# Experts of a mixture layer: the scatter of the block before goes ahead of the gathers three blocks on

## The reference

```python
def step(acc, inp):
    tok, w, e = inp
    xb = xf[tok]
    hid = silu(xb @ wg[e]) * (xb @ wu[e])
    yb = (hid @ wd[e]) * w[..., None]
    acc = acc.at[tok.reshape(-1)].add(yb.reshape(-1, D_MODEL))
    return acc, None
```

## Time and profile before

| | us |
|---|---|
| median of 3 runs | 2062.29 (2060.82 to 2064.68) |
| the profiled execution's own time | 2062.23 |
| its span | 2060.5 |
| PE busy | 1992.8 (97%) |
| DVE busy | 1139.9 (55%) |
| POOL busy | 778.1 (38%) |

### The profile page before, as it was taken

How to read it: one execution, slowest core, us unless ns; L and a number is a source line. 1 busy time by engine, 2 the same in 40 slices (tenths; PEclk the granted TensorE clock), 3 DMA queues, 4 the chain that set the end, 5 groups by cost and what they waited for, 6 DMA issues and landing times.

```text
span 2060.5 us, 23760 instructions
## 1 busy us (share of the span) xinstructions
PE 1992.8 (97%) x7237; PEld 1013.2 (49%) x7238; DVE 1139.9 (55%) x3065; ACT 504.8 (24%) x1102; POOL 778.1 (38%) x717
## 2 busy tenths in 40 slices
PE   8999999999999999999999999999999999999992
PEld 6444667575544444444445554444444444444440
DVE  6222546776621222335676656966666666666645
ACT  3111554452322222314432230111111111111113
POOL 1762005622122221115980002554545545455541
PEclk9999999999999999999999999999999999999996
DMA  5421000011132222144353006999999999999964
GB/s 148 133 86 41 21 21 22 22 47 47 46 129 76 72 82 77 54 123 171 103 207 140 37 31 258 362 361 349 357 359 352 358 358 352 355 349 351 358 206 172
DMA packets 129639, 370.45 MB, mean 180 GB/s; under 512 B 33712, under 2 KB 65668, under 8 KB 103832
## 3 DMA queue, kind: packets, MB, share of 16 engines
q1 hardware_dynamic: 103960, 314.83, 40.8%
q0 software_dynamic: 23520, 54.61, 10.9%
q10 hardware_dynamic: 2080, 0.01, 0.1%
HBM read 320.57 MB, written 68.17 MB: 189 GB/s over the span
## 4 chain that ended last, share of the span: by engine, by line
PE 40%; DMA 7%; POOL 3%; issue 3%; DVE 2%; ACT 0%; SPq 0%; POOLq 0%; DVEq 0%
PE banks L3192 17%; PE banks L3208 8%; DMA sums<-arena,row_to 6%; PE banks L2289 4%; PE banks L2336 3%; POOL arena L2136 2%; PE banks L2014 2%; PE banks L2352 1%; PE banks L279 1%; PE banks L2803 1%; PE banks L2312 1%; PE banks L3200 1%; DMA arena<-in_w_router_dram 0%; DVE arena L3268 0%; DVE arena L3185 0%
## 5 line engine op out<-in xcount | busy, mean ns | idle before, releaser
L3192 PE MATMUL banks<-arena 128*128 128x512 f32 x1056 | 468.8, 597 | 3.3 <-DVE arena L3185 0.8
L3171 POOL DMA_INDIRECT arena<-h_rows,index x268 | 280.0, 1045 | 140.4 <-issue 77.8
L3192 PEld LDWEIGHTS banks<-arena 128*128 128x128 f32 x1056 | 195.2, 190 | 226.3 <-issue 224.8
L1720 PE MATMUL banks<-arena 128*128 128x512 f32 x672 | 299.0, 594 | 1.1 <-ACT arena L323 1.1
L3208 PE MATMUL banks<-arena 128*128 128x512 f32 x528 | 237.6, 593 | 1.3 <-ACT arena L3007 0.8
L3179 POOL DMA_INDIRECT sums<-arena,row_to x66 | 108.0, 1636 | 272.2 <-DMA sums<-arena,row_to 231.9
L3185 DVE STREAM_TRANSPOSE arena<-arena 128x1024 f32<-128x1024 f32 x66 | 133.9, 2029 | 119.8 <-PE banks L3192 115.1
L279 PE MATMUL banks<-arena 128*128 128x512 f32 x416 | 191.8, 598 | 2.5 <-PEq L108 2.2
L1720 PEld LDWEIGHTS banks<-arena 128*128 128x128 f32 x672 | 123.1, 190 | 135.6 <-issue 134.0
L3155 DVE TENSOR_SCALAR index<-row 32x1 uint32<-32x1 f32 x1072 | 155.4, 145 | 17.1
L3208 PEld LDWEIGHTS banks<-arena 128*128 128x128 f32 x528 | 100.2, 190 | 127.0 <-issue 125.3
(11 more groups left out here) (400 smaller groups left out, 2431.9 us busy)
## 6 DMA issues: line engine op xcount, KB each, us to landing
arena<-in_w_exp_gate_dram SPq DMA_DIRECT2D x66, 1024.0 KB
arena<-in_w_exp_up_dram SPq DMA_DIRECT2D x66, 1024.0 KB
arena<-in_w_exp_down_dram SPq DMA_DIRECT2D x66, 1024.0 KB
arena<-in_w_in_dram SPq DMA_DIRECT2D x26, 1024.0 KB, 5.3
gates<-arena SPq DMA_DIRECT2D x60, 256.0 KB, 2.0
arena<-gates SPq DMA_DIRECT2D x15, 1024.0 KB, 7.7
arena<-h_rows,index POOLq DMA_INDIRECT x268
arena<-in_x_dram SPq DMA_DIRECT2D x8, 512.0 KB, 5.8
```

What stands on the lines that cost most here:

```text
L1720: mm = pe.matmul(gate_bank(n, b), left[:, k, :], right[:, k, :], start=(alone and k == 0), stop=(k == 3), skip_group_check=True)
L3171: return pool.indirect_dma_start(w.x[k][:, 256 * q:256 * (q + 1)], None, rows, bass.IndirectOffsetOnAxis(ap=g.index[:, k, q:q + 1], axis=0 ...
L3192: mm = pe.matmul(g.bank[:, 2, :].rearrange("p (a f) -> p a f", a=2), xT[:, k, :], wgu[:, :, k, :], start=(k == 0), stop=(k == KT - 1))
```

## The change

In each step of the experts POOL issues S(c-1) first and G(c+3) after it. Every wait stays with its instruction, and no other engine's order changes.

```diff
             def step(i, c):
+                if has(i, c, -1):
+                    scatter(i, c - 1)
                 if has(i, c, 3):
                     gather(i, c + 3)
-                if has(i, c, -1):
-                    scatter(i, c - 1)
```

## The result

The changed kernel takes 2077.12 us (median of 4 runs, 2074.02 to 2080.53), the kernel before 2062.19 in the same comparison: the ratio is 1.0071, with a 95% interval from 1.0052 to 1.0091. It is slower by 14.9 us. I had predicted +3.2 us and a range that ended at 2071.0.

What follows compares the result with a forecast made beforehand. PE sets the pace with DMA full, and the chains through PE and scatters end almost together. A 5.05 us stop less 1.0, 0.5 and 0.4 gives +3.15 us, predicted 2065.5 us, range 2060.0 to 2071.0.

Steps and rivals of the forecast that it cites:

- the stops don't add up over the blocks: Experts' end: late gathers stop PE for 5.05 us, building up from about block 52; a late PE finds the next gather in place.
- s: How far the scatters move ahead by starting once R(0) is done, carried along the chain: 4.4 us, from 3.3 to 4.8.
- theory D: From the experiments, not the prediction: scatters' chain is slightly slower than PE; the order sets how much PE is spared.
- The floor of the lag: Least time from the start of R(b) to the start of S(b): R's own 0.75 us plus 0.30, some 1.05.
- my own formula: Around block 31: a gather takes the next one's old place, s earlier; T(31) has 8.75 us against a landing of 8.0.
- My first rival: Gathers fall back by nearly a whole step, as s comes out small: slower, +7.5 us, 2069.8; chance 0.34.
- The 0.84 us by which VectorE may be late: Harmless lateness of VectorE, from the hidden product's end at 1624.06 to the transposes at 1624.90; taken off a 5.89 us delay.
- my signs of being wrong: T waits for gathers early, lag of S shrinks under 3 us, T(60) doesn't wait, or steps around 1600 aren't 11.1 us.
- 8.0 us from the end of the last gather's issue to T: Landing time of a gather in full queues, taken near the upper end between 4.5 and 8.84 us.
- the third rival: The scatter chain alone sets the end and gives all of s: faster, -4.4 us, 2057.8; chance 0.06.
- The terms given back: Near the end: 1.0 us at down(59) to up(61), 0.5 slack between R(65) and S(65), 0.4 from weights served sooner.

Runs made afterwards that it cites:

- with the collisions taken away: The changed kernel, with VectorE's selection for block c+4 put ahead of the index work for c+3: 2074.94 us, ratio 1.0056 to the kernel before.
- selection first: The kernel before (old order), with VectorE's selection for block c+4 put ahead of the index work for c+3: 2063.52 us, ratio 1.0004.
- removed in either of two ways: The changed kernel with VectorE's selection put ahead of the index work, 2074.94 us, or with the selection split into four instructions, 2078.32 us.
- The old order with two sums: The kernel before, with odd blocks' scatters to a second sums tensor and each scatter waiting for the one two blocks back: 2062.30 us, ratio 0.9995.

## Why the prediction was wrong

**What bounds the kernel: right, and read too narrowly.** PE and the chain of scatters end almost together. I said so for the tail and used it to cap the gain. What the old trace also said is that the chain runs at 11.18 us per block (S(7) to S(51)) against PE's 11.08 (R(7) to R(51)), and that the old order hides this in a lag that may grow to some 12 us.

**The step that failed: "the stops don't add up over the blocks, since each gather's time hangs on the scatters' chain and not on PE".** The sentence is true of the waits, and I drew from it that the chain would keep its old pace, so that everything after could be read off the old trace, shifted by s. The chain did not keep it: 11.38 us per block after, 11.29 with the collisions taken away, while three kernels with the old order in the loop had 11.18, 11.14 (selection first) and 11.11 (new order at the ends). That is 8.6 of the 11.7 us lost between block 7 and block 51. So a chain that is a little slow by itself, as theory D has it, accounts for the smaller part; the larger is that it runs slower still in the new order. The runs show what it takes: the full weight loads (with five eighths of the down loads the loss is gone), the wait of each scatter for the one before (without it the loss is gone), and more than one gather between the scatter and the next.

**s, the shift of the scatters, was mis-sized.** I took 4.4 us from a range of 3.3 to 4.8. Measured at block 7, the lag shrank from 5.85 to 3.34, by 2.5, and in absolute time S(7) came only 1.3 us earlier. S(1) did start 2.9 us earlier (1315.58 against 1318.46), but took 4.14 us to issue instead of 1.60: line 2649 had held up a gather before (3.42 us at 1314.74), and now held up the scatter. The floor of the lag is 1.6 us, seen at S(1) (1315.58 against R(1) at 1313.98), and not 1.05. By my own formula the gathers of the middle, with 0.75 us to spare at s = 4.4, were then late by more than 1 us, so T had to wait from the start. My first rival named that condition, s below 3.4, and gave it 0.34; its price, +7.5 us, rested on the same unchanged chain and was half of what came. The 0.84 us by which VectorE may be late were too many as well: at 1415.92 the hidden product had ended 0.34 us ahead of the transposes, which started in time, and the matmuls of line 2803 behind them still took 0.75 us more than usual. Two of my signs of being wrong came true: T waited for gathers early, and the lag at block 7 shrank by less than 3 us.

**The room.** Old order: a lag of up to 12 us before PE is stopped. New order: between 1.8 and 6.5 us from block 7 to 51, 3.34 at the first and 4.89 at the last. When the lag grows, a gather comes late, PE is set back, and the lag starts to grow again. From S(35) to S(47) it was 1.8 to 3.5 us, and T waited for none of the gathers behind them, those of blocks 39 to 51. So PE is tied to the scatters in bouts, not block by block, and over the 44 blocks it is spared 3.1 us less drift.

**What held.** I had taken 8.0 us from the end of the last gather's issue to T. At the 19 places where T waited for a gather in the changed kernel it was 7.9 to 8.9 us, 8.3 in the mean. R's waits for landings vanished. The end of the kernel moved with PE and not with the scatters. No gain came, though the chain that ended last ran through the scatters; the third rival was rightly small. The terms given back (1.0, 0.5 and 0.4 us) can't be seen one by one beside a loss of this size, and no run tested them.

**The Trainium skill's rules.** The Trainium skill's "DMA: Bandwidth & Descriptors", section "Rules for kernel authors", says to issue a DMA early and wait for it late; the runs bear it out with a measured slope, +1.6, +6.8 and +14.9 us for one, two and four gathers put behind a wait. The Trainium skill's fit on the same page, section "Anatomy of one DMA", for a DMA from GpSimd gives an estimate of 2.3 us for one gather's bytes. It is not met: the median from issue to landing was 6.7 us in the changed kernel and 5.6 with a quarter of the down loads.

**What stays open.** Why the chain of scatters takes 0.1 us per block more when PE moves in step with it, with the collisions removed (11.29 against 11.18), no run separates. Late weights are hardly the cause: in the changed kernel the three loads of an expert land 9.4, 14.1 and 7.6 us after their issue (medians), and they are issued four blocks, some 45 us, ahead. With the collisions the chain's loss lies in the issues (9.8 us more from S(7) to S(51)); with them removed in either of two ways it lies in landing and restart (426.2 us instead of 419.9). Both pay nearly the same in the end, which looks like a pace that the coupled loop sets and not the scatter alone; that is a guess.

No version tried beats the kernel before by more than its measurement can tell.

## What to carry to other kernels

Where a chain of waits runs at nearly the pace of the bounding engine, ask how far it may fall behind before that engine must wait, and let no reordering use up that room: here 12 us of room hid a chain that was 1% too slow, and some 4 us did not. Do not read the new schedule off the old trace by a shift; once two loops are coupled, the slower one's pace becomes both's, and it may change. An operation whose start hangs on a DMA's landing is a bad thing to put ahead of work that is needed on time.

## What the hardware showed

GpSimd's issue of an indirect DMA is held up by VectorE's selection (tensor_tensor, 128x1024, float32 in, bf16 out, 1.23 us) if it begins while that runs: 2.65 us instead of 1.61. It is not if the issue began before it. The only exception in the changed kernel's trace is S(15), whose issue began 0.03 us into the selection and took 1.62 us. The tensor_tensor of line 2649 (128x3072, float32) held up S(1) in the same way, and in the kernel before a gather, for 3.42 us instead of 1.0. The index work of line 3155 (32x1 each) had no such effect: S(4), issued amid it at 1352.09, took 1.60 us.

TensorE's clock fell for a moment after some short pauses. After, the windows around S(34) (length, busy and count per engine, clock, DMA, GB/s):

```profile
1680.00:1690.00 10.00, 8.97 (x21) 3.61 (x19) 5.39 (x18) 1.07 (x2) 4.46 (x4) 1.00 1.01 367
1690.00:1700.00 10.00, 9.43 (x25) 4.61 (x26) 5.06 (x24) 0.38 (x1) 5.07 (x5) 0.83 1.02 371
```

A granted clock of 0.83 over 10 us means a part of them at the lower level, 1.2 GHz. It followed a pause of 1.28 us before the transposes at 1690.26, and the sixteen up products took 8.48 us instead of 7.11, 1.4 us more. The old order with two sums had one too, behind a wait of 1.66 us for weights:

```profile
1861.27 8.83 PE L3193 MATMUL banks<-arena 128*128 128x512 f32 x16 [1.66 <-DMA arena<-in_w_exp_up_dram]
```

So a pause of 1.3 to 1.7 us on PE can cost as much again. It need not: a pause of 1.47 us before 1302.51 in the changed kernel was followed by none. Its trace had two such falls ahead of the tail, at about 913 and 1692 us, the kernel before none: of the 13.4 us some 1.4 are the second, and the first lies ahead of the experts, where T(0) is already 0.7 us late (1271.13 against 1270.42).
